# RWKV inverses by masked copies and transposes, the end of the RWKV layers by token halves, and one pass for the last low-rank columns

## The chip, the cores and the metric

The kernel runs on one core of one Trainium2 chip. The time is the device time of one execution in microseconds. Three runs of the kernel before gave 1933.72, 1935.93 and 1939.68 us, median 1935.93.

## The reference

Two small transformer blocks run one after the other on 256 tokens of width 1,024, all in float32: four layers, each a token mixer and a gated feed-forward, then two hybrid attention layers. Layers 0 and 3 mix tokens by RWKV-7; the change touches only these.

```python
def rwkv7_time_mix(h, v_first, mix, ...):
    shifted = jnp.pad(h, ((0, 0), (1, 0), (0, 0)))[:, :-1]
    xm = h[:, :, None, :] + (shifted - h)[:, :, None, :] * mix
    r, k, v = ...                                  # three 1024x1024 projections of xm
    decay = jnp.exp(-jnp.exp(logw)); a = jax.nn.sigmoid(a0 + (xa @ a1) @ a2)
    g = jax.nn.sigmoid(xg @ g1) @ g2               # g1: 1024 x 160
    ...                                            # layer 3: v is mixed with layer 0's by v1 (1024 x 32), v2
    def step(state, inp):
        sa = jnp.einsum('bhvk,bhk->bhv', state, kk_t)
        state = (state * w_t[:, :, None, :] - sa[..., None] * (kk_t * a_t)[:, :, None, :]
                 + v_t[..., None] * k_t[:, :, None, :])
        return state, jnp.einsum('bhvk,bhk->bhv', state, r_t)
    y = ((y - mu) * lax.rsqrt(var + RW_GN_EPS)).reshape(B, S, D) * ln_w + ln_b
    y = y + (jnp.sum(rh * kh * r_k, axis=-1, keepdims=True) * vh).reshape(B, S, D)
    out = (y * g).astype(h.dtype) @ w_out
```

There are 16 heads of 64. The kernel does the scan in chunks of 64 tokens, which needs, for each head and chunk, the inverse of a 64x64 unit triangular matrix: 64 inverses per layer.

## The kernel before, in words

Each engine (TensorE, VectorE, ScalarE, GpSimd and the DMA queue on SyncE) has one program in an order written by hand. Engines wait for one another by counting semaphores: `at("dve", key)` is the count at which VectorE has done the step named `key`. Nothing plans the order at run time.

**Weights.** A weight block of 1024x256 comes into a ring of three raw slots. It is worked on in units of 4 x 128 rows: ScalarE rounds a unit to a short float (`hi`, L453), VectorE makes the remainder (`lo`, L463), and TensorE multiplies three times per 128 rows (L401 to L403), so that two short floats stand for one float32. There are four unit buffers: unit u can be rounded once TensorE has finished unit u - 4. A projection onto 256 columns (`full(m, p, g)`) is two units, 48 matmuls.

**Banks.** PSUM has eight banks, handed out in turn by `bank`; TensorE waits until the last user of a bank has read it out.

**Low-rank columns.** The last 32 columns of g1 (and in layer 3 the 32 of v1) are loaded as `tail`. VectorE makes W*mix and W - W*mix, and `pe_lora` runs two f32 matmuls per 128 rows, one on h and one on h shifted by a token (L675, L676), 16 in all, behind `full(0, 1, 1)`.

**Inverses.** `gram` makes 32 products of 64x64 for one half j of the tokens: 'pb', 'bp', 'bq' (a part with rows and columns crossed), later 'kp', 'br', 'kr'. The inverse T and its transpose Tt (`BUF[6]`, `BUF[12]`) grow by doubling through LEVELS 2, 4, 8, 16, 32. In a level, `first_products` multiplies the masked off-diagonal part BM with T (64 products), `second_products` updates T from (Tt, X1) and Tt from (X1, Tt) (64 each; at level 32 only Tt). All are L814. Between them ScalarE copies (L1591) or VectorE subtracts (L2278, L2289), by which of the four groups crosses sides in that level; GpSimd masks the next BM (L2770) and adds identities (L2764). Within the loop over g, TensorE runs a value projection `full(2, 0, g)`, the second products of level g and the first products of the next; ScalarE and VectorE work there on the weight units of the coming projections, and VectorE also on the decay products (L2201, L2208) and the read term (L2214). Then follow 'kp', transposes into token order (`pe_to_tm`, L727: pTM, V, bTM, kTM), level 32, 'br', the products G (L798), 'kr', tp and the `term` sums (L906).

**State loop and end.** Four chunks go through `from_state`, `new_state`, `new_y` in turn, with four `gate` products (L914, L915) among the last. When the y of all 256 tokens is there, four `cen` products (L1023) centre it, ScalarE squares (L1685), four `var` products follow (L1027), ScalarE makes the inverse root by Ln and Exp (L1689, L1691), VectorE multiplies by root and gate and adds the term (L2367, L2370, L2372), ScalarE rounds (L1404) and VectorE makes the remainder (L2060), for one pair of 128-column groups after another. The output projection `pe_out_proj` needs all four pairs in its first block.

## Time and profile before

| what | value |
|---|---|
| median of three runs | 1935.93 us |
| the profiled execution's own time | 1935.0 us |
| its span | 1932.9 us |
| TensorE busy | 1817.4 us, 94% of the span |
| VectorE busy | 1263.3 us, 65% |
| ScalarE busy | 1029.7 us, 53% |
| GpSimd busy | 146.0 us, 8% |
| mean TensorE clock | 0.974 of full |

Busy times come from one profiled execution. A share of the span says little by itself: what a part is worth is read in its own stretch, from the waits that end last there..

### The profile page before, as it was taken

How to read it: one execution, taken by the hardware profiler on the slowest of the kernel's cores; microseconds unless marked ns; L12 is line 12 of the kernel's file. 1: busy time of each engine (PE TensorE's matmuls, PEld its weight loads, DVE VectorE, ACT ScalarE, POOL GpSimd, SP SyncE). 2: the span in 40 equal slices, each digit the busy share in tenths (PEclk: the TensorE clock that was granted, in tenths of full speed). 3: DMA queues.
4: the chain of work that ended last, by engine and by line, in shares of the span. 5: the costliest groups of instructions: out<-in, count | busy, mean ns of one | idle time of the engine just before them, and what ended most of it. 6: DMA issues, size and time to landing. Idle time of an engine off the chain costs nothing.

```text
span 1932.9 us, 43768 instructions
## 1 busy us (share of the span) xinstructions
PE 1817.4 (94%) x18871; PEld 1631.5 (84%) x18871; DVE 1263.3 (65%) x1783; ACT 1029.7 (53%) x1585; POOL 146.0 (8%) x106
## 2 busy tenths in 40 slices
PE   6987999999989999898999999998899999998998
PEld 5887788889979888887698888887798888887887
DVE  6875367865436675486668856876467755775764
ACT  5834455554535554354655545744465554564455
POOL 0051100000000000014000000151100000000000
PEclk9999999999989999899899999999999999998999
DMA  6420145557576655355465562320245555443441
GB/s 190 132 86 4 53 146 184 190 182 244 174 233 217 197 191 180 110 174 178 150 198 184 186 204 93 120 76 4 68 153 191 178 188 169 134 146 104 152 132 66
DMA packets 288535, 287.92 MB, mean 149 GB/s; under 512 B 15240, under 2 KB 286456, under 8 KB 288344
## 3 DMA queue, kind: packets, MB, share of 16 engines
q1 hardware_dynamic: 285048, 284.02, 45.8%
q8 instruction: 150, 2.46, 0.5%
q10 hardware_dynamic: 3296, 1.11, 0.3%
q14 instruction: 41, 0.34, 0.1%
HBM read 284.06 MB, written 1.05 MB: 148 GB/s over the span
## 4 chain that ended last, share of the span: by engine, by line
PE 90%; DVE 4%; issue 3%; ACT 2%; DMA 0%; POOL 0%; SPq 0%; DVEq 0%; ACTq 0%; POOLq 0%
PE ps L419 23%; PE ps L420 12%; PE ps L401 10%; PE ps L403 9%; PE ps L402 9%; PE ps L814 3%; PE ps L436 2%; PE ps L437 2%; PE ps L438 2%; PE ps L713 1%; PE ps L784 1%; PE ps L798 1%; PE ps L675 1%; PE ps L641 1%; PE ps L727 1%
## 5 line engine op out<-in xcount | busy, mean ns | idle before, releaser
L463 DVE TENSOR_TENSOR wl<-raw,wh 128x1024 fp32r<-128x1024 f32 x484 | 596.5, 1251 | 345.4 <-ACT wh L453 340.9
L453 ACT ACTIVATE wh<-raw 128x1024 fp32r<-128x1024 f32 x484 | 499.4, 1041 | 432.0 <-PE ps L420 191.2
L419 PE MATMUL ps<-HH,wh 128*128 128x512 f32 x1408 | 489.7, 391 | 0.0
L420 PE MATMUL ps<-HH,wl 128*128 128x256 f32 x1408 | 397.0, 282 | 0.0
L419 PEld LDWEIGHTS ps<-HH,wh 128*128 128x128 f32 x1408 | 264.3, 188 | 55.6 <-issue 0.4
L401 PE MATMUL ps<-HH,wh 128*128 128x256 f32 x928 | 271.4, 292 | 10.2 <-DVE HH L2498 5.5
L420 PEld LDWEIGHTS ps<-HH,wl 128*128 128x128 f32 x1408 | 266.1, 189 | 0.1
L402 PE MATMUL ps<-HH,wh 128*128 128x256 f32 x928 | 263.6, 284 | 0.0
L403 PE MATMUL ps<-HH,wl 128*128 128x256 f32 x928 | 263.3, 284 | 0.0
L401 PEld LDWEIGHTS ps<-HH,wh 128*128 128x128 f32 x928 | 179.3, 193 | 20.8 <-issue 6.6
L402 PEld LDWEIGHTS ps<-HH,wh 128*128 128x128 f32 x928 | 179.6, 193 | 1.2 <-issue 1.2
L401 PE MATMUL ps<-XH,wh 128*128 128x256 f32 x576 | 166.7, 289 | 13.5 <-DVE XH L2060 13.5
L403 PEld LDWEIGHTS ps<-HH,wl 128*128 128x128 f32 x928 | 179.2, 193 | 0.0
L402 PE MATMUL ps<-XH,wh 128*128 128x256 f32 x576 | 163.4, 284 | 0.0
L403 PE MATMUL ps<-XH,wl 128*128 128x256 f32 x576 | 163.3, 284 | 0.0
L2750 POOL TENSOR_TENSOR B<-B 128x512 f32<-128x512 f32 x20 | 25.9, 1295 | 1345.9 <-ACT B L1400 1345.9
L401 PEld LDWEIGHTS ps<-XH,wh 128*128 128x128 f32 x576 | 111.0, 193 | 18.5 <-DVE XH L2060 12.1
L419 PE MATMUL ps<-XE,wh 128*128 128x512 f32 x336 | 117.0, 390 | 0.0
L402 PEld LDWEIGHTS ps<-XH,wh 128*128 128x128 f32 x576 | 111.1, 193 | 1.0 <-issue 1.0
L403 PEld LDWEIGHTS ps<-XH,wl 128*128 128x128 f32 x576 | 111.1, 193 | 0.0
L1591 ACT ACTIVATE B<-ps 128x512 f32<-128x512 f32 x104 | 58.6, 602 | 75.1 <-PE ps L814 63.7
L420 PE MATMUL ps<-XE,wl 128*128 128x256 f32 x336 | 94.8, 282 | 0.0
(323 smaller groups left out, 3119.6 us busy)
## 6 DMA issues: line engine op xcount, KB each, us to landing
raw<-in_ffn_w_gu_dram SPq DMA_DIRECT2D x88, 1024.0 KB, 5.1
raw<-in_ffn_w_down_dram SPq DMA_DIRECT2D x32, 1024.0 KB, 5.1
raw<-in_w_in_dram SPq DMA_DIRECT2D x32, 1024.0 KB, 5.4
raw<-in_rw_w_rkv_dram SPq DMA_DIRECT2D x24, 1024.0 KB, 5.3
B<-in_w_ada_dram SPq DMA_DIRECT2D x24, 1024.0 KB, 7.7
raw<-in_ds_w_in_dram SPq DMA_DIRECT2D x14, 1024.0 KB, 5.3
raw<-in_ffn_w_down_dram SPq DMA_DIRECT2D x16, 768.0 KB, 4.4
raw<-in_sb_w_qkv_dram SPq DMA_DIRECT2D x12, 1024.0 KB, 5.5
```

Source lines behind the costliest of these rows:

```text
L401: e.matmul(om, h_[:, k, c], xh_, start=m == 0 and k0 + k == 0, stop=False, skip_group_check=True)
L402: e.matmul(om, h_[:, k, c], xl_, start=False, stop=False, skip_group_check=True)
L403: i = e.matmul(om, l_[:, k, c], xh_, start=False, stop=k0 + k == kt - 1, skip_group_check=True)
L419: e.matmul(o[:, m, :], h_[:, k, c], x_, start=k0 + k == 0, stop=False, skip_group_check=True)
L420: i = e.matmul(o[:, m, 0:S], l_[:, k, c], x_[:, 0, :], start=False, stop=k0 + k == kt - 1, skip_group_check=True)
L436: e.matmul(oj, xh_[:, c], h_[:, k, :], start=j == 0 and k0 + k == 0, stop=False, skip_group_check=True)
L437: e.matmul(oj, xl_[:, c], h_[:, k, :], start=False, stop=False, skip_group_check=True)
L438: i = e.matmul(oj, xh_[:, c], l_[:, k, :], start=False, stop=k0 + k == KD - 1, skip_group_check=True)
L453: e.activation(wh[:, u % UNITS, 0:kn * 256], raw[:, j % RAW, k0 * 256:(k0 + kn) * 256], ACT.Copy).then_inc(*up("hi"))
L463: e.tensor_tensor(wl[:, u % UNITS, 0:kn * 256], raw[:, j % RAW, k0 * 256:(k0 + kn) * 256], wh[:, u % UNITS, 0:kn * 256].bitcast(F32), ALU. ...
L814: i = e.matmul(o[half(b), p_ * HD:p_ * HD + HD], L[half(a), g[0], g[1], p_, :], Rr[half(a), g[0], g[1], p_, :], start=True, stop=True, ski ...
L1591: e.activation(dst, PS(*key)[:, :], ACT.Copy, scale=scale).then_inc(*up("act", key))
```

## The change

**Low-rank columns.** `tail` now holds W - W*mix and W*mix side by side. One pass of eight f32 matmuls over h gives both products ('gt'); ScalarE copies them out; after `full(0, 1, 2)` two matmuls with the identity add the second to the first, shifted by a token ('gv').

**Inverses.** Only one matrix is kept per level, in `BUF[6]`, laid out by head with the two chunk parities side by side (`GQ`). ScalarE fills it with minus the identity (`clear`), and VectorE writes the below-diagonal blocks of each level into it by masked copies straight from PSUM (`copy_predicated` with an int32 mask `low8(m)`). The transpose is made on TensorE (`turned`, 16 transposes of 128x128 per level) and copied out by ScalarE. First products use the unmasked Gram matrix 'bp' (`At`); the crossed Gram product 'bq' and the separate update of Tt are gone, and so are all of GpSimd's masks and identity additions. At level 32 the first products go by masked copies into `BUF[0]`, filled with the identity before. The last read projection and the value projections are cut in two halves by unit (`block_halves`, its sum in bank 0, while `bank` hands out the other seven).

**Order.** In TensorE's loop a level is: first products, transposes, half a value projection, second products, other half. 'kp' moves into level 32, 'br' behind pTM, 'kr' behind V, bTM ahead of G. On VectorE, `key_decay` and `read_decay` swap and `own_term` moves by half a step.

**End.** Gates 0 and 1 move ahead of the second pair's key products. Centring, variance, root, weighting, rounding and remainder are done for the first 128 tokens from the end of the third y on, beside the last chunk, and then for the other 128, in operations of half the width on VectorE and in the rounding. Each centring and variance product now covers four column groups of 128 tokens, 512 columns.

```diff
+    for m in (1, *LEVELS):
+        add(f"low{m}", (sc // (2 * m) == tc // (2 * m)) & (sc % (2 * m) >= m) & (tc % (2 * m) < m))
...
+            def block_halves(m, p, g):
+                key, free = ("full", n, m, g), ("dve", ("vmix", n, g)) if n and m == 2 else ("act", ("full", n, m, g))
+                ready = [[("dve", ("xml", n, m, k // 2))] for k in range(KD)] if g == 0 else None
+                o = kept_bank(e, 0, key, free)
+                for k0, kn, u in next_units(KD):
+                    fm_unit(e, key, o, KD, k0, kn, u, parts_of(*((HH, HL), (XH, XL))[p]), ready)
+                    yield
             pe_lora(e, ("wa", n), down, down_mixed, 0, 128, h, ("dve", ("lora", n, 3)), ("dve", ("lora", n, 4)))
...
+            e.wait_ge(*at("dve", ("lora tail", n)))
+            for k in range(KD):
+                e.wait_ge(*at("dve", ("h", n, k)))
+                i = e.matmul(o[0:2 * tw, 0:S], tail[:, k, 0:2 * tw], h[:, k, :], start=k == 0, stop=k == KD - 1, skip_group_check=True)
+            i.then_inc(*up("mm", ("gt", n)))
             full(0, 1, 2)
+            o = bank(e, ("gv", n), ("act", ("gv", n)))
+            e.wait_ge(*at("act", ("gt", n)))
+            e.matmul(o[0:tw, 0:S], ident[0:2 * tw, 0:tw], lor[0:2 * tw, :], start=True, stop=False, skip_group_check=True)
+            e.matmul(o[0:tw, 1:S], ident[0:2 * tw, tw:2 * tw], lor[0:2 * tw, 0:S - 1], start=False, stop=True,
+                     skip_group_check=True).then_inc(*up("mm", ("gv", n)))
             R_, Kp, v_, Bt_, Pm, term = FM(10), FM(7), FM(13), FM(8), FM(9), FM(4)
             V, pTM, bTM, kTM = TM(2), TM(3), TM(1), TM(8)
-            T, Tt, X1, BM, Lk, KR, BR, Un = GR(6), GR(12), GR(11), GR(0), GR(14), GR(11), GR(9), GR(0)
+            T, Tw, X1, Xw, At = GQ(6), GQ(12), GQ(11), GQ(0), GQ(1)
...
+            def turned(m, j):
+                for r in range(2):
+                    o = bank(e, ("turn", n, m, j, r), ("act", ("turn", n, m, j, r)))
+                    for q in range(4):
+                        i = e.transpose(o[:, q * P:q * P + P], BUF[6][:, (8 * j + 4 * r + q) * P:(8 * j + 4 * r + q) * P + P], ident)
+                    i.then_inc(*up("mm", ("turn", n, m, j, r)))
...
-                    quarters("xs", m, pair, straight, lambda g: side(m, g), BM, T, product_by)
+                for j in range(2):
+                    for a in range(2):
+                        e.wait_ge(*at("act", ("bp", n, j, a)))
+                        e.wait_ge(*at("dve", ("low", n, m // 2, j, a)))
+                    quarters("xs", m, j, At, T, "dve" if m == 32 else "act")
+                for j in range(2):
...
+                for j in range(2):
+                    for a in range(2):
+                        e.wait_ge(*at("dve" if m == 32 else "act", ("xs", n, m, j, a)))
+                        e.wait_ge(*at("act", ("turn", n, m // 2, j, a)))
+                    if m == 32:
+                        quarters("tt", m, j, Xw, Tw, "act")
+                    else:
+                        quarters("low", m, j, Tw, X1, "dve")
+            cur["first"] = 1
             for j in range(2):
                 gram("pb", j, Pm, Bt_)
             for j in range(2):
                 gram("bp", j, Bt_, Pm)
...
+            last_read = block_halves(0, 1, 3)
+            next(last_read)
...
+            next(last_read)
             for g in range(4):
-                full(2, 0, g)
+                first_products(LEVELS[g])
+                values = block_halves(2, 0, g)
+                next(values)
                 second_products(LEVELS[g])
-                if g < 3:
-                    first_products(LEVELS[g + 1])
+                next(values)
+            first_products(32)
             for j in range(2):
                 gram("kp", j, Kp, Pm)
+            second_products(32)
+            cur["first"] = 0
             for j in range(2):
                 pe_to_tm(e, ("pTM", n, j), Pm, j)
+            for j in range(2):
+                gram("br", j, Bt_, R_)
             e.wait_ge(*at("dve" if n else "act", ("vmix", n, 3) if n else ("full", n, 2, 3)))
             for j in range(2):
                 pe_to_tm(e, ("V", n, j), v_, j)
-            first_products(32)
             for j in range(2):
-                gram("br", j, Bt_, R_)
-            second_products(32)
+                gram("kr", j, Kp, R_)
+            for j in range(2):
+                pe_to_tm(e, ("bTM", n, j), Bt_, j)
             for j, par in groups:
                 e.wait_ge(*at("act", ("V", n, j, 1)))
...
             new_state(1)
             new_y(1)
+            gate(0)
+            gate(1)
             keys_values(1, 1)
             y_values(1)
             from_state(2)
             new_state(2)
             new_y(2)
-            gate(0)
-            gate(1)
+            centred(0)
             from_state(3)
+            spread(0, 0)
+            spread(0, 1)
+            new_y(3)
             gate(2)
-            new_y(3)
+            centred(1)
+            spread(1, 0)
+            spread(1, 1)
+            cur["bank"] += 1
             gate(3)
...
+            def clear(j):
+                e.wait_ge(*at("dve", ("rn read", n, j)))
+                e.activation(BUF[6][:, j * 1024:j * 1024 + 1024].rearrange("p (q t) -> p q t", t=HD),
+                             C("eye").unsqueeze(1).to_broadcast([P, 16, HD]), ACT.Copy, scale=-1.0).then_inc(*up("act", ("minus eye", n, j)))
...
+            clear(1)
+            tw = 32 + 32 * n
+            e.wait_ge(*at("mm", ("gt", n)))
+            e.wait_ge(*at("mm", ("a2", n, 3)))
+            e.activation(lor[0:2 * tw, :], PS("gt", n)[0:2 * tw, 0:S], ACT.Copy).then_inc(*up("act", ("gt", n)))
+            hi(e)
+            evac(0, 2, R_)
...
+            def quarters_out(key, m, j, dst, scale=1.0):
+                for a in range(2):
+                    e.wait_ge(*at("mm", (key, n, m, j, 1)))
+                    e.activation(dst[:, j, :, a, :], q8(PS(key, n, m, j, a)[:, :]), ACT.Copy, scale=scale).then_inc(*up("act", (key, n, m, j, a)))
+            def turned(m):
+                for j in range(2):
+                    for r in range(2):
+                        copy_out(("turn", n, m, j, r), Tt[:, j, r, :])
...
+            evac(0, 3, R_)
             for g in range(4):
+                for j in range(2):
+                    quarters_out("xs", LEVELS[g], j, X1)
+                hi(e, 1)
+                turned(LEVELS[g] // 2)
                 hi(e, 1)
                 if n == 0:
                     evac(2, g, v_)
...
             log_and_exp(e)
+            turned(16)
+            for j in range(2):
+                quarters_out("tt", 32, j, Tn, -1.0)
             for j in range(2):
                 to_tm(("pTM", n, j), pTM[:, j, :])
             for j in range(2):
...
             negate_u(0)
             y_out(0)
             negate_u(1)
             y_out(1)
+            gate(0)
             negate_u(2)
+            gate(1)
             y_out(2)
-            gate(0)
-            gate(1)
+            squares(0)
             negate_u(3)
+            spread(0, 0)
+            spread(0, 1)
+            y_out(3)
+            rounded_y(0, 0)
+            rounded_y(0, 1)
             gate(2)
-            y_out(3)
+            squares(1)
+            rounded_y(0, 2)
+            spread(1, 0)
+            spread(1, 1)
...
+            def level(key, m, dst):
+                for j in range(2):
+                    for a in range(2):
+                        e.wait_ge(*at("mm", (key, n, m, j, 1)))
+                        e.copy_predicated(dst[:, j, :, a, :], low8(m), q8(PS(key, n, m, j, a)[:, :])).then_inc(*up("dve", (key, n, m, j, a)))
+            lo(e)
             lo(e)
             for g in range(4):
...
+                if n and g:
+                    value_mix(g - 1)
                 lo(e, 1)
                 if g == 0:
+                    key_decay(0)
+                    key_decay(1)
+                if g == 1:
                     read_decay(0)
                     read_decay(1)
...
+                if g > 1:
+                    own_term(g - 2)
+                level("low", LEVELS[g], T)
+                lo(e, 1)
+            if n:
+                value_mix(3)
+            e.wait_ge(*at("act", ("eye", n)))
+            level("xs", 32, Xw)
             for j, par in groups:
                 masked("kp", j, par, Lk, "mU")
...
             e.wait_ge(*at("dve", ("state", n, 0)))
             next_state(1)
+            gate_term(0)
             negate_u(2)
             e.wait_ge(*at("dve", ("state", n, 1)))
             next_state(2)
-            gate_term(0)
             gate_term(1)
             negate_u(3)
+            weighted(0, 0)
+            weighted(0, 1)
+            gated(0, 0)
+            gated(0, 1)
+            rest_y(0, 0)
+            rest_y(0, 1)
             gate_term(2)
+            weighted(0, 2)
+            gated(0, 2)
+            for g in range(3):
+                weighted(1, g)
+            rest_y(0, 2)
+            gated(1, 0)
+            gated(1, 1)
+            rest_y(1, 0)
+            gated(1, 2)
+            rest_y(1, 1)
             gate_term(3)
...
```

## Rows read from the trace of the kernel before

**Rows 1.** page, parts 1 and 4: busy time by engine; the chain by engine

```profile
...
PE 1817.4 (94%) x18871; PEld 1631.5 (84%) x18871; DVE 1263.3 (65%) x1783; ACT 1029.7 (53%) x1585; POOL 146.0 (8%) x106
...
PE 90%; DVE 4%; issue 3%; ACT 2%; DMA 0%; POOL 0%; SPq 0%; DVEq 0%; ACTq 0%; POOLq 0%
...
```

**Rows 2.** busy time by stretch: length, engines with instructions, clock, DMA share, GB/s

```profile
...
91.88:203.04 111.16, 91.88 (x3066) 85.37 (x3065) 70.75 (x79) 49.02 (x77) 40.37 (x26) 0.97 0.15 47
1246.23:1356.01 109.78, 93.97 (x3081) 87.43 (x3081) 76.07 (x91) 49.60 (x81) 41.01 (x26) 0.98 0.15 48
233.19:244.14 10.95, 7.04 (x18) 2.88 (x16) 5.77 (x10) 9.31 (x16) 0.00 (x0) 1.00 0.89 287
1396.39:1423.44 27.05, 26.10 (x193) 25.81 (x193) 17.67 (x24) 13.00 (x18) 2.12 (x2) 0.84 0.30 98
...
```

**Rows 3.** by line, layer 0's middle: count | busy, mean ns | idle before

```profile
...
L814 PE MATMUL ps<-B 64*64 64x64 f32 x1792 | 33.4, 226 | 13.1 <-issue 12.1 <-DVE B L2278 0.9
...
L784 PE MATMUL ps<-B 64*64 64x64 f32 x704 | 13.3, 232 | 6.0 <-issue 6.0
...
```

**Rows 4.** TensorE's waits in layer 3's middle: total, times, longest

```profile
...
PE ps L814 <- issue: 8.9, 8, 1.6
...
```

**Rows 5.** timeline of TensorE, layer 0: start, length, [idle before]

```profile
...
120.11 3.10 PE L814 MATMUL ps<-B 64*64 64x64 f32 x126 [2.46 <-issue]
...
134.54 2.38 PE L814 MATMUL ps<-B 64*64 64x64 f32 x126 [1.02 <-issue]
137.81 2.20 PE L814 MATMUL ps<-B 64*64 64x64 f32 x126 [0.89 <-issue]
...
193.44 2.09 PE L784 MATMUL ps<-B 64*64 64x64 f32 x128
195.47 1.97 PE L727 MATMUL ps<-CT,B 128*128 128x128 f32 x16
...
```

**Rows 6.** DMA queues from 117.5 to 118.7: packets, MB, share

```profile
...
q8 instruction: 1, 0.02, 5.7%
...
```

**Rows 7.** page, part 3: the same queue over the span

```profile
...
q8 instruction: 150, 2.46, 0.5%
...
```

**Rows 8.** busy by stretch: three levels, a projection, low-rank, G, gates, projection, transposes

```profile
...
108.76:156.64 47.88, 38.95 (x1302) 37.08 (x1296) 35.43 (x32) 18.50 (x28) 21.50 (x13) 0.96 0.19 61
108.76:114.55 5.79, 5.79 (x55) 5.66 (x49) 5.68 (x4) 1.71 (x3) 5.79 (x4) 1.00 0.01 3
79.02:86.03 7.01, 7.01 (x33) 3.44 (x32) 6.94 (x7) 6.61 (x8) 0.00 (x0) 1.00 0.00 0
187.28:191.55 4.27, 4.08 (x142) 3.88 (x134) 0.69 (x1) 2.39 (x4) 0.00 (x0) 1.00 0.02 4
222.70:226.28 3.58, 3.58 (x19) 2.95 (x16) 1.26 (x3) 1.44 (x3) 0.00 (x0) 1.00 0.02 5
1264.87:1272.22 7.35, 7.35 (x50) 7.22 (x49) 1.68 (x2) 1.97 (x4) 4.07 (x3) 0.77 0.25 89
172.80:176.65 3.85, 3.85 (x38) 3.47 (x33) 1.65 (x3) 3.15 (x7) 0.00 (x0) 1.00 0.02 4
...
```

**Rows 9.** timeline of ScalarE in layer 0's first level

```profile
...
111.92 1.06 ACT L453 ACTIVATE wh<-raw 128x1024 fp32r<-128x1024 f32 x1 [2.41 <-PE ps L403]
...
115.80 0.60 ACT L1591 ACTIVATE B<-ps 128x512 f32<-128x512 f32 x1 [0.55 <-PE ps L814]
...
```

**Rows 10.** timeline of VectorE, layer 0

```profile
...
64.35 0.42 DVE L2054 TENSOR_TENSOR B<-B 128x256 f32<-128x256 f32 x1
...
83.37 2.35 DVE L463 TENSOR_TENSOR wl<-raw,wh 128x1024 fp32r<-128x1024 f32 x2
...
107.86 0.69 DVE L2278 TENSOR_TENSOR B<-CT,ps 128x512 f32<-128x512 f32 x1 [3.42 <-PE ps L814]
...
139.38 4.53 DVE L2201 TENSOR_TENSOR B<-B 128x1024 f32<-128x1024 f32 x2
...
```

**Rows 11.** timeline of VectorE, layer 0's end

```profile
...
248.61 1.47 DVE L2060 TENSOR_TENSOR XH<-B,XH 128x512 fp32r<-128x512 f32 x2
```

More of the change, by code:

```diff
@@ L190, in two, with low8 @@
             return ap.rearrange("p (k t) -> p k t", k=2)
+        def low8(m):
+            return C(f"low{m}").bitcast(I32).unsqueeze(1).to_broadcast([P, 8, HD])
         def q8(ap):
@@ L340, in bank, with kept_bank @@
             return PSB[i]
+        def kept_bank(e, i, key, *free):
+            for ev in bank_free.get(i, ()):
+                e.wait_ge(*at(*ev))
+            bank_free[i], bank_of[key] = free, i
+            return PSB[i]
         def kept_pair(e, r, key, *free):
```

323 lines of the change are left out of this document (119 added, 204 removed).

## The prediction

> **What bounds the kernel now.** The page first: TensorE is busy for 94% of the span, and 90% of the chain that ended last is its work [rows 1]; time goes only where TensorE works less or waits less. Then the stretches that the change touches, one per RWKV layer. What I call the middle runs from the first Gram product to the last `term` product: 111.16 us in layer 0 and 109.78 in layer 3, with TensorE busy for 91.88 and 93.97 [rows 2]. So 19.3 and 15.8 us are idle. The view by lines says what ends that idle time: 12.1 + 6.0 us of it in layer 0 end with "issue", which is no semaphore [rows 3], and so do 8.9 us before L814 alone in layer 3 [rows 4]. After it come the state loop and the end: centring, variance, gate, output projection. In layer 0, 10.95 us pass from 233.19 to 244.14 with TensorE busy for 7.04; in layer 3 the projection takes 27.05 us at a mean clock of 0.84 of 2.4 GHz [rows 2].
>
> **What the "issue" waits are.** 64x64 products run at full rate until TensorE stops for 2.46 us before 120.11 [rows 5], and in just that gap a transfer of the instruction queue runs [rows 6]. That queue moved 150 transfers [rows 7]; 18,871 matmuls and as many weight loads [rows 1] make 252 TensorE instructions in each. 64 f32 products of 64x64 take 2.09 us and are 128 matmul records [rows 5], with their loads 256 instructions: one transfer's worth. Dense runs of 126 records begin at 134.54 and 137.81, 3.3 us apart, each behind such a wait [rows 5]. I read it so: one block of 256 is fetched ahead, a fetch needs about 3.4 us, and a dense block (2.1 us) costs 1.3 or so of waiting unless slow instructions lie in it. The Trainium skill says otherwise (Runtime: NRT & Kernel Launch, Instruction fetch mechanics): TensorE's buffer holds 2,048 instructions and fetching is hidden behind the issue rate. By that rule fewer instructions return nothing; here the row is against it, and what it would make of the time is rival D.
>
> **The middle: work.** In products of 64x64 (2.09 us for 64), per layer. Before: 11 Gram products of 32, and in the inverses 5 x 64 first and 4 x 128 + 64 second products, 896, which are the 1,792 records of L814 [rows 3]. After: the crossed Gram product goes (-1.05 us), second products are 5 x 64 (-256 products, -8.4), and 80 transposes of 128x128 come in, 16 in 1.97 [rows 5] (+9.85). Sum +0.4 us: TensorE's own work does not shrink. Instructions do, by 1,152 - 160, almost four blocks; and each level now has two separate runs of 64 products with 16 transposes or half a projection (half of 5.79 us [rows 8], 2.93 with the hand-over) between them, so that slow instructions lie in nearly every block. I let the fetch waits of the four levels go.
>
> **The middle: the new wait.** In a level ScalarE copies out the first products, rounds one weight unit (`hi(e, 1)`), and only then copies the transposes. That unit's buffer comes free when the level's own first half projection is done: before, it starts at 111.92, 0.23 us after it, takes 1.06, and a copy takes 0.60 [rows 9], the next 0.49 more. TensorE runs the half projection behind the transposes and the second products right behind that, so these wait 0.23 + 1.06 + 0.60 + 0.49 = 2.4 us, and all of TensorE's queue behind them. A level: 2.1 (first) + 1.97 + 2.93 + 2.4 + 2.1 (second) + 2.93 = 14.4, say 14.5. Before: three levels in 47.88 [rows 8], 16.0 each.
>
> VectorE must fit in: weight remainder (1.2), two decay products (1.22 each; 4.53 for both now, while GpSimd works too), four masked copies [rows 10]. No row has a masked copy (`copy_predicated`). Below, nothing beats L2278, 128x512 out of PSUM with a mask-like second operand: 0.69 alone, 0.61 in a row; above, twice that. I take 0.61, the nearest row. With t the end of the first half projection: unit t+1.3, remainder t+2.5, decay t+4.95, copies for j=0 t+6.2, for j=1 t+7.4; TensorE asks for them at t+7.4 and t+8.5. It just fits. GpSimd's masks and identities leave; no wait names them, so 0.
>
> **The middle, layer 0.** The last low-rank columns take 7.01 us [rows 8]; half of the passes stay (3.5) and two identity products come in (0.9). But the next projection's weight remainder is made from 83.37 on, ready at 84.6 [rows 10], so that projection starts there, not at 82.5, and the Gram products could start at 91.4 instead of 91.88. The first needs the bank of that projection (ScalarE has it copied at 92.3), the second pair that of the low-rank result, behind a sigmoid table load (94.0): Gram products end at 97.3, the last read projection at 103.2. Level one has 0.8 more: its last transposes take the bank of the first product, which ScalarE empties only after filling BUF[0] with the identity (2.0 for 2,048 columns, from 0.60 for 512 and 1.06 for 1,024 [rows 9]). It ends at 118.4, three more at 162. The rest: 2.1 first, 2.0 transposes, 4.2 kp and second, 7.9 for four sets of transposes, 4.2 br and kr, 4.27 G [rows 8], 2.1 tp, 3.5 term = 30.2; one fetch wait of 1.4 (kp and second are 512 dense instructions in a row), 0.5 for evacuations: 32.1. End 194.3 against 203.04: **-8.7**.
>
> **Layer 3.** Start 1245.9, Gram products to 1251.9, half projection 1254.8, `v2` (eight matmuls like those of gates 0 and 1, 3.5 [rows 8]) 1258.3, half 1261.2. Here banks bite: the second pair of first products needs the bank of `v2` 0 and the transposes those of 1 to 3, emptied by eight sigmoids (about 0.43 each) that stand on ScalarE behind a weight unit that waits for the second half; the last transposes stand behind these and the identity fill: +4.5. Then 14.4 + three levels of 14.5 and 32.1: end 1355.9 against 1356.01: **0**.
>
> **The end.** Token halves double the instructions: 128x256 on VectorE takes 0.42, 0.69 at 512 [rows 10]. Gates 0 and 1 (3.46 of the 3.58 us [rows 8]) move ahead of T, the end of the third y product: a shift. In the written order: variance products of half 0 end T+5.4, ScalarE's roots T+7.4, last y out T+8.0, rounding of pairs 0 and 1 to T+8.7, gate 2 and squares of half 1 to T+10.75, VectorE's pair 2 T+11.65 and its rounding T+12.05, and only then the roots of half 1, T+13.4 and T+14.65. From there each pair needs 0.9 (two operations), 0.38 (rounding), 0.42 (remainder), and VectorE is the queue: remainders done at T+15.5, 16.6, 18.75 and, with gate 3 before it, 21.85. Before, T = 222.70 and the last remainder ends at 250.08 [rows 11], T+27.4. Less the gates that moved, 21.85 + 3.46 - 27.4 = **-2.1** per layer; the projection's second unit waits for pair 3 in both. The state loop has two fetch waits (0.7, 0.9); gates among its products spread the instructions, **-0.5** per layer. The low clock in the projection cost 0.8 and 1.5 us; TensorE is still mostly idle from T+14 to T+22, so I count none of it back.
>
> Sum: -8.7 + 0 - 2 x 2.6 = -13.9 on the profiled execution's own 1935.0 (span 1932.9): 1921. The median of the runs shown is 0.9 higher, and one dip of the clock in the new waits is likely (in 1264.87 to 1272.22 a projection takes 7.35 instead of 5.79 [rows 8]: 1.5): **1923**.
>
> **Rivals.**
> A. ScalarE's copies of the transposes are not late, and the levels close up to TensorE's work: -2.4 x 8 = -19 more, 1903. Against: the written order. 0.10.
> B. A masked copy costs 1.22 in a row: j=1 comes at t+9.8 for t+8.5, 1.3 late in eight levels, and some 4 at the first and last: +14, 1936. For: a mask, a source and old values to keep. Decides from 0.9 us per copy. 0.13.
> C. Transposes and waits together pull the clock down: 1.5 us per level, +12, 1935. Against: 3.85 us full of transposes at a clock of 1.00 [rows 8]; for: no idle time stood beside those. 0.07. The Trainium skill has a rule for it (TensorE: Matmul & The Clock Gate, Part 4: PE-mode transpose): a transpose doesn't count as activity for the clock.
> D. The "issue" time is no fetching and stays (18.1 and most of 15.8), and ScalarE's wait comes on top in eight levels: 1935 - 5 (the end) + 19 + 5 (banks of layer 3) = 1954 with no overlap, 1943 if half of it overlaps. Slower; decides once more than two thirds of the idle time stays. 0.08.
> E. New waits for banks and buffers eat most of the gain: 1930 to 1934. 0.10.
> The forecast's own case, 1914 to 1930: 0.52.
>
> **How the numbers follow.** Within 0.3%, 5.8 us, a measurement of this kernel can't tell a change. Faster: the forecast, A, a little of E: 0.66; same: B, most of C and E, a tail of the forecast: 0.24; slower: D and bits of B and C: 0.10. The range 1908 to 1936 leaves out A and D.
>
> **What would show it.** "Issue" before L814 and L784 below 5 us per layer in the middles; instruction transfers down from 150 to about 142; eight new waits of about 2.4 us before second products, ended by ScalarE's copies; masked copies of 0.69 us; the low-rank stretch 4.4 instead of 7.0 with most of it lost to the weight remainder. I am wrong if "issue" stays, if masked copies pass 0.9, or if layer 3 gains as much as layer 0.

## The result, and the profile after

The changed kernel takes 1946.05 us (median of 4 runs, 1944.51 to 1946.57) beside 1937.11 for the kernel before: a ratio of 1.0059, 95% interval 1.0043 to 1.0074. It is slower by 0.6%, where 1923 us were forecast. The profiled execution took 1945.65 us, with a span of 1943.7.

The page of the changed kernel, parts 1, 3 and 4, beside [rows 1] and [rows 7]:

```profile
PE 1819.1 (94%) x17855; PEld 1632.0 (84%) x17855; DVE 1219.8 (63%) x1783; ACT 1045.6 (54%) x1625; POOL 68.2 (4%) x58
...
q8 instruction: 142, 2.33, 0.5%
...
PE 87%; ACT 5%; DVE 5%; issue 2%; DMA 1%; POOL 0%; SPq 0%; DVEq 0%; ACTq 0%; POOLq 0%
```

TensorE has 1,016 fewer matmuls and is as busy as before, and the instruction queue moves 142 transfers, as forecast. What changed hands is the chain: ScalarE had 2% of it and has 5%. Now the stretches that answer to [rows 2] (layer 0's middle, layer 3's middle, layer 3's output projection), and layer 0's output projection; the columns are length, busy time with instructions of TensorE, its loads, VectorE, ScalarE, GpSimd, then the granted clock:

```profile
92.36:201.27 108.91, 92.25 (x2570) 85.58 (x2572) 45.86 (x63) 53.95 (x90) 1.83 (x2) 0.97 0.15 48
1244.68:1369.52 124.84, 104.18 (x2586) 95.49 (x2588) 53.43 (x74) 54.44 (x92) 1.83 (x2) 0.91 0.12 41
1408.31:1435.40 27.09, 24.87 (x193) 24.42 (x194) 17.07 (x29) 13.71 (x21) 2.28 (x2) 0.94 0.65 213
...
239.36:264.71 25.35, 24.56 (x193) 24.16 (x193) 17.07 (x29) 13.71 (x21) 2.12 (x2) 0.93 0.69 228
```

The loss is in one row. Layer 3's middle grew from 109.78 to 124.84 us; layer 0's, the same instructions, shrank from 111.16 to 108.91. In layer 3 TensorE's busy time rose by 10.2 us for the same work at a clock of 0.91 instead of 0.98, and its idle time by 4.9 (20.7 for 15.8). The waits of TensorE in layer 3, from the low-rank pass to the last term product, say what the idle time is now; before, it was issue ([rows 4]):

```profile
PE ps L823 <- ACT B L1628: 9.9, 4, 2.5
PE ps L799 <- ACT lor L1618: 2.8, 1, 2.8
PE ps L389 <- DVE wl L456: 2.3, 1, 2.3
PE ps L832 <- ACT B L1637: 2.1, 1, 2.1
PE ps L799 <- issue: 2.0, 2, 1.3
PE ps L832 <- DVE B L2319: 1.5, 1, 1.5
PE ps L823 <- issue: 1.4, 1, 1.4
PE ps L389 <- DVE B L2277: 1.4, 3, 0.5
```

L823 are the products of the inverses, L832 the transposes, L799 the Gram products, L389 the projections. The first row is the forecast wait behind `hi(e, 1)`: four times 2.5 us, and four more in layer 0. This is one of them, on ScalarE's and TensorE's timeline of layer 3:

```profile
1289.38 1.06 ACT L446 ACTIVATE wh<-raw 128x1024 fp32r<-128x1024 f32 x1 [4.33 <-PE ps L391]
1290.35 2.05 ACT L1628 ACTIVATE B<-ps 128x512 f32<-128x512 f32 x4
1291.77 3.41 PE L823 MATMUL ps<-B 64*64 64x64 f32 x128 [2.49 <-ACT B L1628]
```

ScalarE stood idle for 4.33 us, rounded a weight unit that was not urgent, and only then copied the transposes that had long been there. And the 64 products that followed took 3.41 us, not 2.1: TensorE's clock fell 0.4 us after they began. Two of these falls, behind the first and the last of the four waits; then two levels of layer 3, all of its four levels, and the four of layer 0:

```profile
1275.10:1278.51 3.41, 3.41 (x128) 3.41 (x128) 3.40 (x4) 0.57 (x2) 0.00 (x0) 0.50 0.02 5
1326.30:1329.71 3.41, 3.41 (x71) 3.29 (x72) 2.91 (x5) 0.00 (x0) 0.00 (x0) 0.50 0.03 5
...
1281.63:1314.99 33.36, 27.48 (x642) 25.98 (x641) 18.17 (x26) 12.43 (x20) 0.00 (x0) 0.90 0.20 65
...
1262.19:1331.83 69.64, 55.27 (x1281) 52.06 (x1280) 34.08 (x47) 29.82 (x50) 0.00 (x0) 0.90 0.13 42
...
105.33:168.45 63.12, 52.02 (x1282) 49.57 (x1281) 27.99 (x38) 27.88 (x45) 0.00 (x0) 0.95 0.15 46
```

A fall is 3.4 us at the lower level (1.2 GHz instead of 2.4) and costs 1.7 us of work. In layer 3 one begins 0.0 to 1.2 us behind each of the four waits (the waits end at 1275.06, 1291.77, 1308.44, 1325.12; the falls begin at 1275.1, 1292.2, 1309.2, 1326.3), and three more lie in that middle; before there was one. Of the three, the one at 1244.4 stands at the end of the wait of 2.8 us in front of the Gram products, and the one at 1346.8 behind waits of 1.45 and 0.72 us. The one at 1258.0 stands behind no wait: the longest idle time in the 12 us before it is 0.64 us, 8 us earlier, and what TensorE did just before are the 16 `v2` products, which read 32 partitions. The single fall of layer 3's middle before, at 1264.9, stands behind the same products. The kernel after, then the kernel before:

```profile
1253.93 3.72 PE L868 MATMUL ps<-lor,v_rows 32*128 32x256 f32 x16
```

```profile
1261.22 3.71 PE L859 MATMUL ps<-lor,v_rows 32*128 32x256 f32 x16
```

In eleven of the twelve traces of this case a fall begins within 1.3 us of the end of these products; the filled wait, below, is the exception. So idle time is not the only thing with a fall behind it. Six more falls than before, at 1.7 us, are the 10.2 us of busy time. In layer 0 only two of the four waits have a fall behind them (at 131.6 and 162.4).

The whole difference by stretches, in us against the kernel before, from the first instruction of each stage in both traces:

| stretch | forecast | measured |
|---|---|---|
| layer 0, to the last term product | -8.7 | -1.8 |
| layer 0, state loop and end | -2.6 | -4.0 |
| from there to layer 3's RWKV | 0 | +2.2 |
| layer 3, to the last term product | 0 | +17.0 |
| layer 3, state loop and end | -2.6 | -1.6 |
| rest | 0 | -1.0 |
| sum | -13.9 | +10.8 |

### The profile page after: what moved, and what is told of

Read it like the earlier page. It is cut to its first block, busy times and chain, and to the rows that moved or that the text cites. A ratio compares the mean times of both kernels' runs of the same rounds, so it can differ in the third digit from the quotient of the medians.

```text
span 1943.7 us, 41674 instructions
## 1 busy us (share of the span) xinstructions
PE 1819.1 (94%) x17855; PEld 1632.0 (84%) x17855; DVE 1219.8 (63%) x1783; ACT 1045.6 (54%) x1625; POOL 68.2 (4%) x58
## 4 chain that ended last, share of the span: by engine, by line
PE 87%; ACT 5%; DVE 5%; issue 2%; DMA 1%; POOL 0%; SPq 0%; DVEq 0%; ACTq 0%; POOLq 0%
PE ps L412 23%; PE ps L413 12%; PE ps L389 10%; PE ps L391 9%; PE ps L390 9%; PE ps L823 2%; PE ps L429 2%; PE ps L430 2%; PE ps L431 2%; PE ps L708 1%; PE ps L799 1%; PE ps L722 1%; ACT wh L446 1%; PE ps L808 1%; PE ps L636 1%
## 5 line engine op out<-in xcount | busy, mean ns | idle before, releaser
L456 DVE TENSOR_TENSOR wl<-raw,wh 128x1024 fp32r<-128x1024 f32 x484 | 586.0, 1228 | 416.4 <-ACT wh L446 411.4
L389 PE MATMUL ps<-HH,wh 128*128 128x256 f32 x928 | 271.9, 293 | 13.1 <-DVE HH L2559 6.2
L389 PEld LDWEIGHTS ps<-HH,wh 128*128 128x128 f32 x928 | 178.9, 193 | 23.7 <-issue 4.9
L389 PE MATMUL ps<-XH,wh 128*128 128x256 f32 x576 | 166.4, 289 | 14.5 <-DVE XH L2111 6.5
L389 PEld LDWEIGHTS ps<-XH,wh 128*128 128x128 f32 x576 | 110.5, 192 | 19.3 <-issue 5.9
L429 PE MATMUL ps<-wh,HH 128*128 128x256 f32 x256 | 75.2, 294 | 0.0
L412 PEld LDWEIGHTS ps<-XE,wh 128*128 128x128 f32 x336 | 63.1, 188 | 13.2
```

What stands on the lines that cost most here:

```text
L389: e.matmul(om, h_[:, k, c], xh_, start=m == 0 and k0 + k == 0, stop=False, skip_group_check=True)
L412: e.matmul(o[:, m, :], h_[:, k, c], x_, start=k0 + k == 0, stop=False, skip_group_check=True)
L429: e.matmul(oj, xh_[:, c], h_[:, k, :], start=j == 0 and k0 + k == 0, stop=False, skip_group_check=True)
L456: e.tensor_tensor(wl[:, u % UNITS, 0:kn * 256], raw[:, j % RAW, k0 * 256:(k0 + kn) * 256], wh[:, u % UNITS, 0:kn * 256].bitcast(F32), ALU. ...
```

## The experiments

Ratios are to the kernel before, in runs on the same chip; the changed kernel's is 1.0059. The experiments ran on four chips, on which the kernel before took 1933.8 to 1936.6 us, so versions are compared by their ratios, and differences in us between two versions are worked out from these. Each has one trace.

**One order on ScalarE.** In each level the copies of the transposes go ahead of the weight unit:

```diff
-                hi(e, 1)
                 turned(LEVELS[g] // 2)
                 hi(e, 1)
+                hi(e, 1)
```

> The changed kernel with one order swapped on ScalarE: in each of the eight levels it copies the transposes out before it rounds the first weight unit, so that the second products need not wait 2.48 us for that unit (8 x 2.48 = 19.8 us in the trace of the changed kernel). Theory W (the lost time is these waits, and the falls of the granted clock come from them: seven falls of 1.7 us each in layer 3, two in the levels of layer 0): waits before the second products below 0.5 us, the falls inside the levels gone (six of them, -10 us), but VectorE's masked copies, which stand behind a weight remainder and two decay products, come about 1.2 us late in each level (+10): 1926 us. Rival T (the clock falls because of the transposes themselves, 16 per level, waits or not): the waits go and the falls stay, at 1.7 us for each level of layer 3: 1934 to 1936 us.

Measured: 1924.56 us, ratio 0.9952 (0.9935 to 0.9968), 1.1% below the changed kernel. One line moved in an order turns the loss into a gain. Two levels of layer 3, then its middle, and the two longest waits of TensorE from the first level on:

```profile
1271.06:1297.99 26.93, 24.67 (x641) 23.32 (x641) 17.89 (x27) 12.86 (x21) 0.00 (x0) 1.00 0.26 81
1236.69:1347.67 110.98, 98.72 (x2586) 90.09 (x2588) 52.78 (x74) 54.59 (x92) 1.85 (x2) 0.96 0.14 46
```

```profile
PE ps L823 <- DVE B L2319: 2.6, 3, 1.5
PE ps L832 <- ACT B L1637: 2.1, 1, 2.1
```

No wait on L1628 is left and no fall lies in these two levels: 13.5 us per level instead of 16.7. What is late next is VectorE's masked copy (L2319), as expected.

**The wait kept, TensorE kept busy in it.** This tells whether the falls come from the waits or from the transposes. Ten products that compute nothing of use are issued ahead of the wait, and for that the banks are taken ahead of it too:

```diff
+FILL = 10
...
+                    os = [bank(e, (key, n, m, j, a), ("act" if m == 32 else "dve", (key, n, m, j, a))) for a in range(2)]
+                    if m < 32 and j == 0:
+                        for r in range(FILL):
+                            e.matmul(os[0][:, :], HH[:, 0:P], HH[:, 0:512], start=True, stop=True, skip_group_check=True)
                     for a in range(2):
                         e.wait_ge(*at("dve" if m == 32 else "act", ("xs", n, m, j, a)))
...
```

> The changed kernel, with ten matmuls of 128 x 512 that compute nothing of use issued by TensorE ahead of the wait for the transposes' copies, in each of the eight levels (about 2.2 us of work inside the 2.48 us of waiting; they write a bank that the second products then overwrite). The waits on the path keep their length, only TensorE is busy in them. Theory W (idle time beside the transposes lowers the clock): no fall of the granted clock in the levels, those of layer 3 at 14.5 to 15 us instead of 16.7, all in all six falls of 1.7 us less: 1936 us. Rival T (the transposes alone lower it): falls as before, level pitch 16.7 in layer 3, 1946 us or some us more because the filling delays the second products.

Measured: 1933.66 us, ratio 0.9999 (0.9986 to 1.0011). Useless work made the changed kernel 0.6% faster, 11.6 us; the RWKV layers' traces, from the low-rank stretch to the output projection, show eleven falls without it and four with it, and seven at 1.7 us are 11.9. (The two profiled executions lie 14.1 us apart; outside these layers their falls differ too, so that the two sums meet so closely is partly chance.) None of the four lies in the levels. Two levels of layer 3, and one filled wait:

```profile
1276.88:1306.90 30.02, 29.08 (x661) 26.77 (x660) 18.05 (x26) 12.39 (x20) 0.00 (x0) 1.00 0.23 73
```

```profile
1284.36 2.45 PE L851 MATMUL ps<-HH 128*128 128x512 f32 x10
```

The path is as long as before (2.45 us stand where 2.48 were waited) and a level takes 15.0 us, for 16.7.

**The same, filled with transposes.** Is a transpose work for the clock?

```diff
-FILL = 10
+FILL = 18
...
-                            e.matmul(os[0][:, :], HH[:, 0:P], HH[:, 0:512], start=True, stop=True, skip_group_check=True)
+                            e.transpose(os[0][:, r % 4 * P:r % 4 * P + P], BUF[6][:, r % 8 * P:r % 8 * P + P], ident)
```

> The changed kernel with its 2.48 us waits before the second products filled by 18 transposes of 128x128 that compute nothing of use (about 2.2 us by 0.123 us each), where the kernel with the filled wait had ten matmuls. The path keeps its length. Theory W1 (only idle time lowers the clock, a transpose is work like any other): as with matmuls, no fall of the granted clock in the levels, ratio to the kernel before 1.000. Rival W2, which is the rule of the Trainium skill (TensorE: Matmul & The Clock Gate, Part 4: PE-mode transpose) that transposes don't count as activity: then the filled wait is idle time for the clock, the falls of 1.7 us stay or come in more levels, layer 3's levels at 16.7 us or more: ratio 1.006 to 1.010.

Measured: 1929.40 us, ratio 0.9976 (0.9964 to 0.9987).

```profile
1274.56:1304.70 30.14, 28.45 (x677) 27.17 (x676) 18.06 (x26) 12.40 (x20) 0.00 (x0) 1.00 0.22 73
```

```profile
1282.04 2.13 PE L851 MATMUL ps<-CT,B 128*128 128x128 f32 x18
1284.48 0.74 PE L824 MATMUL ps<-B 64*64 64x64 f32 x34 [0.31 <-ACT B L1634]
```

34 transposes in each level and no fall in any of the eight: W2 falls, and in this kernel the transposes kept the clock up as well as products did. W1 says more, that only idle time lowers the clock, and that isn't shown: this trace, too, has a fall (at 1252.1) behind the `v2` products.

**The end undone.** The changed kernel with centring, variance, roots and roundings over all tokens again (the three functions' ends taken from the kernel before).

> The changed kernel with the end of both RWKV layers put back to what it was (gates after the third y product, centring and variance over all tokens after the last y, one pass of roots, products and roundings). Theory: from the traces the end by token halves gained 4.1 us in layer 0 and 1.6 in layer 3 (from the last term product to the first product of the next stage: 67.5 to 63.4, and 68.7 to 67.1), so this kernel is 5.7 us slower than the changed one: 1952 us. Rival: the gain in these stretches came with the fetch waits and the clock, not with the halves, and the kernel is within 2 us of the changed one: 1945 to 1948.

Measured: 1952.53 us, ratio 1.0100 (1.0083 to 1.0117), about 8 us slower than the changed kernel (3 to 12 by the two intervals). In the traces the two ends, from the last term product to the first product of the next stage, take 66.9 and 67.5 us here and 63.4 and 65.7 in the changed kernel: 5.2 us, what the end by token halves was forecast to gain. The rest lies outside the ends; one more fall in the middle of layer 0 is part of it.

**The low-rank columns alone,** on top of the kernel before.

> The kernel before with one part of the change alone: the last low-rank columns with factor and shifted part side by side in one pass, then two products with the identity. Theory: it gives nothing or costs a little, because the next projection waits for its weight remainder on VectorE anyway and the bank of the result stays behind the sigmoid's table load; in the traces the stretch from the second read projection to the first Gram product went from 12.8 to 12.9 us in layer 0 and from 12.8 to 15.4 in layer 3: 1937 to 1940 us. Rival: each layer gains the 2.6 us by which the pass is shorter (7.0 to 4.4): 1932.

Measured: 1933.80 us, ratio 1.0002 (0.9988 to 1.0017). Nothing. The pass is 3.35 us shorter (3.66 instead of the 7.01 of [rows 8]), but the next projection waits for its weight remainder all the same, for 2.1 us in this kernel's trace as in the changed kernel's, which these lines show:

```profile
83.42 2.35 DVE L456 TENSOR_TENSOR wl<-raw,wh 128x1024 fp32r<-128x1024 f32 x2
```

```profile
84.78 0.36 PE L389 MATMUL ps<-XH,wh 128*128 128x256 f32 x1 [2.10 <-DVE wl L456]
```

**VectorE's order too.** On top of the first experiment, the masked copies go first in each level:

```diff
             for g in range(4):
-                if n and g:
-                    value_mix(g - 1)
+                level("low", LEVELS[g], T)
                 lo(e, 1)
...
-                level("low", LEVELS[g], T)
+                if n:
+                    value_mix(g)
                 lo(e, 1)
```

> The kernel with the transposes' copies first on ScalarE, and on VectorE in each level the four masked copies ahead of the weight remainder, the decay products and the value mix. In the trace with the transposes first, TensorE waits 1.15, 1.61, 0.47, 0.46 us in layer 0 and 1.54, 0.48, 0.57, 0.61 in layer 3 for the last masked copy (6.9 in all). Theory: a masked copy is cheap (0.61 to 0.73) and only its place behind the remainder makes it late, so these waits go: about 6.5 us less than with the transposes first, ratio to the kernel before 0.992 instead of 0.9952. Rival: the freed time comes back as fetch waits, since a level then takes 12 us for 640 TensorE instructions (2.5 blocks of 256, 8.5 us at 3.4 us each): under 3 us less, ratio 0.994 or more.

Measured: 1918.11 us, ratio 0.9906 (0.9890 to 0.9922), 9 us below the first experiment by the ratios (4 to 13 with their intervals): the theory's 6.5 or better, and not the rival. Two levels of layer 3 take 25.10 us, 12.55 each, of which TensorE works 12.3:

```profile
1263.30:1288.40 25.10, 24.58 (x641) 23.27 (x640) 18.50 (x24) 12.42 (x20) 0.00 (x0) 1.00 0.18 52
```

So whatever is behind the "issue" waits, it does not bound a level of 640 instructions in 12.5 us.

**The instructions behind the levels reordered.** On top of the first experiment: the transposes of the first operand between kp and the last second products, those of the values ahead of br.

> The kernel with the transposes' copies first, and only the order of TensorE's work behind the last level changed: the 16 transposes of the first operand go between the kp products and the last second products, those of the values ahead of the br products, so that no more than 128 products of 64x64 stand in a row. The instructions and their dependencies are the same. In the trace with the transposes first, waits that end with issue stand in this stretch at 0.86 in layer 0 (and one of 1.7 us before the value transposes) and at 0.81, 1.33 and 1.17 in layer 3. Theory (instruction fetch: a block of 256 needs about 3.4 us, a dense block runs in 2.1): these waits shrink by some 2 us per layer, -3 to -4 us in all, ratio 0.9935. Rival (they have another cause, or the blocks only wait somewhere else, as the instructions stay the same in number): within 1 us, ratio 0.995.

Measured: 1924.87 us, ratio 0.9949 (0.9933 to 0.9966): no difference, and a fault of the experiment. With the value transposes moved ahead, br and kr stood side by side, 512 instructions again, and the waits went there: in layer 3 the 1.17 us in the last second products became 0.91 and 1.67 in br and kr. It tells nothing against fetching and is no proof of it. ScalarE's copies of the first operand moved along with the transposes.

**All of it together.** Transposes first, masked copies first, the reordered tail; and in front of the levels the low-rank result leaves its bank by a plain copy, `v2` stands behind both halves of the projection, and the identity fill of 2 us moves to where ScalarE is idle:

```diff
-            e.activation(sg[0:32, 1, :], PS("gv", n)[0:32, 0:S], ACT.Sigmoid).then_inc(*up("act", ("gv", n)))
+            e.activation(lor[0:tw, :], PS("gv", n)[0:tw, 0:S], ACT.Copy).then_inc(*up("act", ("gv", n)))
...
+            e.activation(sg[0:32, 1, :], lor[0:32, :], ACT.Sigmoid)
...
                 turned(LEVELS[g] // 2)
                 hi(e, 1)
+                if g == 0:
+                    e.activation(BUF[0][:, :].rearrange("p (q t) -> p q t", t=HD), C("eye").unsqueeze(1).to_broadcast([P, 32, HD]),
+                                 ACT.Copy).then_inc(*up("act", ("eye", n)))
                 hi(e, 1)
```

> All of it together: transposes' copies first, masked copies first, the tail spread, and in front of the levels: the low-rank result leaves its bank by one plain copy (the sigmoid, with its table load of 1.28 us, reads that copy later), the v2 products stand behind both halves of the last read projection, and the identity fill of 2.0 us on ScalarE stands in the first level where the engine is idle. Theory: from 0.9952 with the transposes first, masked copies -6.5 us, tail -3.5, in layer 3 the waits of 2.77 (bank behind the table load), 0.94 and 2.12 (banks behind sigmoids and fill) go, in layer 0 those of 0.76 and 0.6, so -7, and the two falls of the clock there go with them (-3.4): 1925 - 20 = 1905 us, ratio 0.985. Rival: what is taken away here comes back as fetch waits and as the weight remainder's lateness: half of it, 1915, ratio 0.990.

Measured: 1914.58 us, ratio 0.9888 (0.9870 to 0.9905). The rival came true: of 20 us below the first experiment 12 were had, and 9 of these the masked copies alone had given (0.9906; the two intervals overlap). Much of what was taken away came back as a wait that ends with "issue". The Gram products of layer 3 in this kernel, and the instruction queue from 1236.7 to 1240.0:

```profile
1233.11 3.60 PE L799 MATMUL ps<-B 64*64 64x64 f32 x229 [0.95 <-ACT lor L1616]
1240.05 0.68 PE L799 MATMUL ps<-B 64*64 64x64 f32 x27 [3.34 <-issue]
```

```profile
q8 instruction: 1, 0.02, 1.9%
```

The wait for the bank fell from 2.77 to 0.95 us, and the dense products ran into 3.34 of issue, in layer 0 into 3.46. One transfer of instructions runs in the gap, as in the kernel before ([rows 6]). In the changed kernel it was 0.64 at this place, behind the longer wait for the bank. It varies between versions that have the same order here: the kernel of the last experiment below is one, and there it is 3.81 in layer 3 and 2.09 in layer 0.

**The dense runs set apart.** Same instructions, same number, another order: half of a projection between the two pairs of Gram products, and behind the levels 64 products and 16 transposes by turns. One weight remainder on VectorE moves with that half, ahead of the first masked copies:

```diff
+            last_read = block_halves(0, 1, 3)
+            next(last_read)
             for j in range(2):
                 gram("bp", j, Bt_, Pm)
-            last_read = block_halves(0, 1, 3)
-            next(last_read)
             next(last_read)
...
                 gram("br", j, Bt_, R_)
             for j in range(2):
-                gram("kr", j, Kp, R_)
-            for j in range(2):
                 pe_to_tm(e, ("bTM", n, j), Bt_, j)
+            for j in range(2):
+                gram("kr", j, Kp, R_)
...
+            lo(e)
             for j, par in groups:
                 e.wait_ge(*at("act", ("minus eye", n, j)))
...
             lo(e)
-            lo(e)
             for g in range(4):
```

> The kernel with everything fixed, and only TensorE's dense 64x64 work set apart: one half of the last read projection goes between the two pairs of Gram products in front of the levels (and its weight remainder ahead of the first masked copies), and behind the levels every 64 products (2.1 us) alternate with 16 transposes: kp, transposes, second, transposes, br, transposes, kr. The number of instructions is the same. In the trace with everything fixed, waits that end with issue stand at 3.46 in the Gram products and 1.84 + 0.96 behind the levels in layer 0, at 3.34 and 0.87 + 1.19 in layer 3: 11.7 us. Theory (fetch: 256 instructions run in 2.1 us where they are dense and take about 3.4 us to come; 256 + 32 in 4.1 us do not outrun it): these fall below 3 us in all, the kernel gains 6 to 9 us: ratio 0.9845 (0.9888 with everything fixed). Rival (as in the first try, where the waits moved and the time stayed): ratio 0.988 to 0.989.

Measured: 1906.08 us, ratio 0.9849 (0.9830 to 0.9869), as the theory gave. The same Gram products:

```profile
1229.63 2.10 PE L799 MATMUL ps<-B 64*64 64x64 f32 x128 [0.95 <-ACT lor L1616]
...
1234.66 1.38 PE L799 MATMUL ps<-B 64*64 64x64 f32 x76
1236.72 1.03 PE L799 MATMUL ps<-B 64*64 64x64 f32 x52 [0.68 <-issue]
```

3.34 us have become 0.68 here, and 3.46 none in layer 0. Behind the levels little changed: 1.58 and 0.62 in layer 0, 1.33 and 0.86 in layer 3, so 4.4 us for 4.9, where the theory had under 3 in all. Most of the gain is in front of the levels, and some of it is the clock's: the two layers' traces have six stretches at the lower level with everything fixed and four here. This is the fastest version: 1.5% below the kernel before, 2.1% below the changed one.

**The dense runs joined.** On the kernel with everything fixed: kp, second products, br and kr in one run.

> The opposite: the kernel with everything fixed, but kp, the last second products, br and kr stand in one run of 256 products of 64x64 (1,024 instructions) behind the transposes of the first operand. Theory (fetch): four blocks in 8.4 us of work need 13.6 us, less one fetched ahead: issue waits of 4 to 5 us in this run in each layer, for 2.8 and 2.1 with everything fixed: +4 us, ratio 0.991. Rival (issue waits do not depend on how dense the run is): 0.9885 to 0.989.

Measured: 1915.63 us, ratio 0.9896 (0.9875 to 0.9916); the intervals overlap with 0.9888, so the time decides nothing. In the trace layer 0 has 1.58 + 1.82 + 1.55 = 5.0 us of issue there, as the theory has it (4 to 5). Layer 3 has only 0.80 + 1.36, beside 1.58 and 0.72 of waits for VectorE and ScalarE under which a fetch could run on.

## Why the prediction was wrong

**The reading of before was right.** "Issue" all but vanished from the levels: 0.7 us in the four levels of layer 0 and none in layer 3's. Transfers came down from 150 to 142, and where half of a projection was put between two dense runs the waits went (3.34 to 0.68, 3.46 to none; the nine traces with the dense order have 1.0 to 3.5 us there in layer 0). That it is fetching which fills them is read from the transfers in two of the gaps and from their number; no run tells it from another cause that goes with dense runs.

**The new wait was right, and mis-ranked.** 2.4 us were forecast before second products in all eight levels, ended by ScalarE's copies; 2.48 were measured. The masked copies took what was bounded: four in layer 3's first level, on VectorE's timeline:

```profile
1277.17 1.32 DVE L2319 COPY_PREDICATED B<-CT,ps 128x512 f32<-128x512 int32 x2
1278.79 1.35 DVE L2319 COPY_PREDICATED B<-CT,ps 128x512 f32<-128x512 int32 x2 [0.29 <-PE ps L823]
```

0.66 to 0.68 us each in pairs, and 0.72 for the mean duration of one in layer 0's levels, so rival B, which decides from 0.9, falls.

**The step that failed is rival C:** "transposes and waits together pull the clock down", at 7 in 100, with "one dip of the clock in the new waits is likely: 1.5" in the sum. In the traces there is one fall behind each of the four waits in layer 3's levels, two behind layer 0's, and three more in layer 3's middle. The price of one was right (1.5 us forecast, 1.7 measured), the number was not: the two middles have nine, 15.3 us where the sum had 1.5. These 13.8 us are more than half of the 23.2 between the forecast change (-13.9 and the one dip, -12.4) and the measured one (+10.8); the other terms stand below. Without them even rival C's own number, 1935, is 11 us short. Rival C was right about the waits and wrong about the transposes. Against it stood one row, 3.85 us of transposes at full clock; the filling with transposes shows that this row was right about transposes, and it said nothing of waits. The evidence on waits was in front of me: the two falls in layer 0's middle of the kernel before stand where TensorE had been waiting ([rows 5] has 2.46 us before 120.11, and a fall begins at 121.5 in that trace; the other begins at 97.6, in a wait of 2.45). The row from which I took the price, 1264.87 to 1272.22, shows the one that doesn't: it stands behind the `v2` products. I had counted the new wait as 2.4 us each and should have asked what a wait costs besides its own length. The time lies among rival D's numbers (1943 to 1954), but not by its mechanism: the issue waits did go.

**Terms that were mis-sized.** Levels: 58.7 us forecast for layer 0's four, 63.1 measured, of which 3.4 are falls; 62.4 for layer 3's, including 4.5 for banks, 69.6 measured. Here the banks' share was 0.93 + 2.12, less than forecast; 4 falls cost 6.8 and the value mix, whose last operation holds the bank of the half projections, three times 0.45. In front of the levels I had let only the fetch waits of the four levels go and given the Gram products none, though 128 of them are 512 dense instructions: 2.32 us in layer 0. In layer 3 the wait for the low-rank result's bank was 2.77 us behind a table load, where the forecast's Gram products had 1.8 for all their waits (6.0 us from 1245.9 to 1251.9, less 4.2 of work). Behind the levels: 32.1 forecast, 32.8 in layer 0, 37.7 in layer 3 (issue 2.75 for 1.4, a fall, and 2.9 of waits for evacuations for 0.5). The low-rank stretch was sized right at 4.4 "with most of it lost".

**The end was right, the sum partly by luck:** the last remainder was forecast at T+21.85 and came at T+22.25 and T+22.3; 5.2 us forecast, 5.6 in the traces, about 8 by undoing it. But 2.1 of the 5.6 are the two output projections, in which TensorE's busy time went from 25.27 to 24.56 and from 26.10 to 24.70 us with less time at the lower clock. The forecast had counted nothing back there.

**Not foreseen:** 2.2 us of lead melt between the RWKV layers. In the stretch up to the second feed-forward block TensorE now waits on a transfer of modulation weights:

```profile
PE ps L708 <- DMA B<-in_w_ada_dram: 3.4, 1, 3.4
```

Before, the wait at this place was 1.4 us for ScalarE. It looks as if work that starts earlier meets a transfer that doesn't; no experiment tested this, and one trace speaks against it: with the masked copies first the work starts earlier still, and the wait is 1.4 us for ScalarE again. So the cause stays open.

**Open:** why a fall follows every wait in layer 3's levels and only two of four in layer 0's. Levels, waits and work are alike but for the value mix. The filled waits show that without idle time there is no fall in the levels; they don't say which waits make one, nor why the `v2` products have a fall behind them without any.

## What to carry to other kernels

A wait of TensorE has two prices: its length, and half of what it does in the 3.4 us after it if the clock falls; where waits repeat in a loop, count the second for each of them until a trace shows otherwise (in this kernel it came behind six of eight), and test it by filling the wait with useless products. When an operand is produced by another engine, put its evacuation ahead of that engine's prefetch work unless the prefetch is due sooner: here that order on ScalarE was worth 1.1%, more than the 0.7% that the whole change was forecast to bring. And look at how TensorE's small instructions are strewn, not only at how many there are: here 128 products of 64x64 in a row came with an "issue" wait of 1.0 to 3.5 us in layer 0 in all nine traces with this order, and in the one with half of a projection between them with none (0.68 in layer 3).

## What the runs showed of the hardware

Falls of the clock came behind six of eight waits of 2.5 us, though TensorE worked for most of the time around them (27.5 of 33.4 us in two levels of layer 3). In place of the wait, 18 transposes of 128x128 (2.13 us) kept them away like 10 products of 128x512 (2.45 us). And falls came without a wait: in eleven of twelve traces one begins within 1.3 us of the end of the 16 `v2` products on 32 partitions (3.7 us), with no wait over 1 us in the 8 us before it. The Trainium skill (TensorE: Matmul & The Clock Gate, Part 4: PE-mode transpose) says that a transpose doesn't count as activity for the clock; this kernel's measurement goes against it. A predicated copy of 128x512 from PSUM with an int32 mask takes 0.72 us on VectorE on average (16 in layer 0's levels) and 0.66 in a pair, about as much as a plain subtraction of that size ([rows 10] has 0.69 for one alone). And an "issue" wait of 3.34 us stands in 128 products of 64x64 (256 matmul records) where nothing slower lies among them, and 0.68 us where half of a projection does, with the instructions unchanged. If it is fetching, as the transfer in the gap suggests, the Trainium skill's rule (Runtime: NRT & Kernel Launch, Instruction fetch mechanics), that fetching is hidden behind the issue rate, does not hold for products this short.
